# Two transformer blocks on one core: the state space mixer computed transposed, channels on the partitions

## The reference, cut to what matters

```
xbc = silu(conv4(xbc) + conv_b)                  # per channel, along the tokens
xs, bm, cm = split(xbc, [1024, 256])             # 16 heads of 64 channels; 2 groups
dt = softplus(dtb + dt_bias);  a_neg = -exp(a_log)
y = ssd(xs, dt, a_neg, bm, cm)                   # for each head: (C B^T * decay) @ (xs * dt)
y = y + d_skip[:, None] * xs                     # one D for each head
y = y * silu(zb)                                 # the gate z, 1024 channels
y = rmsnorm over each group of 512 channels, eps 1e-5, times norm_g
```

## Time and profile before

| what | us |
|---|---|
| median of three runs | 2783.86 |
| the profiled execution | 2783.81 |
| its span, first to last instruction | 2782.0 |
| PE busy (share of the span) | 2761.5 (99%) |
| DVE busy | 1822.0 (65%) |
| ACT busy | 1464.6 (53%) |
| POOL busy | 239.3 (9%) |

### The profile page before, as it was taken

How to read it: one execution, slowest core, us unless ns; L and a number is a source line. 1 busy time by engine, 2 the same in 40 slices (tenths; PEclk the granted TensorE clock), 3 DMA queues, 4 the chain that set the end, 5 groups by cost and what they waited for, 6 DMA issues and landing times.

```text
span 2782.0 us, 44672 instructions
## 1 busy us (share of the span) xinstructions
PE 2761.5 (99%) x18116; PEld 2471.4 (89%) x18116; DVE 1822.0 (65%) x2860; ACT 1464.6 (53%) x2398; POOL 239.3 (9%) x187
## 2 busy tenths in 40 slices
PE   9999999999999999999999999999999999999998
PEld 8989889989989889989888987899899888878997
DVE  6656676646656666656568777765565687787755
ACT  6445555545455655444456566445454566655452
POOL 0010011010010010010014100110100131001100
PEclk9999999999999999999999999999999999999999
DMA  6544445555544345555555444555555554445653
GB/s 247 197 168 163 149 156 191 190 188 192 202 171 149 139 172 205 202 185 203 195 189 182 139 171 153 212 197 197 191 201 191 182 188 152 160 159 184 217 193 125
DMA packets 75068, 504.09 MB, mean 181 GB/s; under 512 B 8784, under 2 KB 10480, under 8 KB 19184
## 3 DMA queue, kind: packets, MB, share of 16 engines
q1 hardware_dynamic: 74576, 501.07, 50.7%
q10 hardware_dynamic: 288, 0.17, 0.0%
HBM read 500.12 MB, written 1.08 MB: 180 GB/s over the span
## 4 chain that ended last, share of the span: by engine, by line
PE 92%; DVE 5%; POOL 2%; ACT 1%; issue 1%; DMA 0%; SPq 0%; DVEq 0%; ACTq 0%
PE ps L1570 45%; PE ps L1589 39%; PE ps L1610 3%; POOL wlo L2496 2%; DVE wlo L2038 1%; DVE conv L2325 1%; PE ps L1705 1%; PE ps L1703 1%; PE ps L1730 1%; ACT whi L1781 0%; ACT conv L1949 0%; PE ps L1720 0%; PE ps L1721 0%; PE ps L1722 0%; DVE ps L2142 0%
## 5 line engine op out<-in xcount | busy, mean ns | idle before, releaser
L1781 ACT ACTIVATE whi<-raw 128x1024 fp32r<-128x1024 f32 (+3 forms) x938 | 975.9, 1043 | 636.8 <-PE ps L1570 428.8
L2038 DVE TENSOR_TENSOR wlo<-raw,whi 128x1024 fp32r<-128x1024 f32 (+2 forms) x894 | 1083.8, 1219 | 257.5 <-ACT whi L1781 256.5
L1589 PE MATMUL ps<-xT_both,whi 128*128 128x256 f32 x6592 | 824.2, 278 | 1.0 <-DVE v_mla L2252 1.0
L1589 PEld LDWEIGHTS ps<-xT_both,whi 128*128 128x128 f32 x6592 | 783.1, 188 | 8.3 <-issue 6.9
L1570 PE MATMUL ps<-whi,xT_both 128*128 128x512 f32 (+2 forms) x2336 | 628.6, 391 | 2.9 <-DVE xT_both L2061 1.6
L1570 PEld LDWEIGHTS ps<-whi,xT_both 128*128 128x128 f32 x2336 | 425.3, 188 | 84.2 <-issue 9.3
L1589 PE MATMUL ps<-xT_both,wlo 128*128 128x256 f32 x3296 | 442.5, 277 | 0.0
L1589 PEld LDWEIGHTS ps<-xT_both,wlo 128*128 128x128 f32 x3296 | 405.8, 188 | 0.0
L1570 PE MATMUL ps<-wlo,xT_both 128*128 128x512 f32 (+2 forms) x1168 | 354.4, 384 | 0.3 <-DVE wlo L2038 0.3
L1570 PEld LDWEIGHTS ps<-wlo,xT_both 128*128 128x128 f32 x1168 | 218.3, 188 | 43.7 <-DVE wlo L2038 1.4
L1570 PE MATMUL ps<-whi,hT_hi 128*128 128x512 f32 x704 | 221.4, 390 | 0.0
(11 more groups left out here) (310 smaller groups left out, 2210.9 us busy)
## 6 DMA issues: line engine op xcount, KB each, us to landing
raw<-in_w SPq DMA_DIRECT2D x435, 1024.0 KB, 4.8
vr<-in_vrows SPq DMA_DIRECT2D x19, 512.0 KB, 6.1
raw<-in_w SPq DMA_DIRECT2D x12, 768.0 KB, 4.3
raw<-in_w SPq DMA_DIRECT2D x10, 896.0 KB, 4.5
sums<-scratch SPq DMA_DIRECT2D x8, 512.0 KB, 4.5
raw<-in_w SPq DMA_DIRECT2D x4, 832.0 KB, 4.5
raw<-in_w SPq DMA_DIRECT2D x4, 576.0 KB, 3.7
raw<-in_w SPq DMA_DIRECT2D x4, 512.0 KB, 6.9
```

Source lines behind the costliest of these rows:

```text
L1589: made = e.matmul(out, ws[:, o:o + 128], xs[:, kt, :], start=kt == 0 and n == 0 and c % 2 == 0, stop=kt == job.nk - 1 and n == 2, skip_gro ...
L1781: e.activation(out, raw, ACT.Copy).then_inc(*mark("hi", i))
L2038: e.tensor_tensor(out, raw, hi.bitcast(F32), sub).then_inc(*mark("lo", i))
```

## The change

The state space branch stays with channels on the partitions from the convolution to the branch product. The order of the pieces changes: the first chunk of va opens the stage, z follows xbc and is computed in the form `columns`. `ssd` swaps its operands: 64 columns of `xd` are stationary and the decay tiles are streamed, 256 and 128 columns, two heads on the two column halves. D comes in on ACT by channel (`conv_d`), the POOL multiplication by D is gone. The sum of squares over 512 channels now runs over partitions and tiles: ACT squares (`ssd_square`), DVE adds the tiles of a group (`ssd_add`), PE multiplies by a 128x128 tile of 1/512 so that each partition holds the mean of each of 256 tokens (`ssd_mean`), DVE adds eps, POOL takes the power of -0.5 of that 128x256 tile, DVE multiplies the group's 128x1024 of `ob` by it. Group 0 is done at steps s = 12 and 13 of the chain, group 1 in `last_norm` after the last piece of va. `to_T` of `ob` is replaced by `halve_b`, which has no transposes.

```diff
-        for n in (0, 1):
-            gemm(("z", l, n), (l,), 8, [(w, ZB + 512 * n, ZB + 512 * n + 512)])
+        gemm(("va", l, 0), (l,), 8, [(w, VA, VA + 512)])
...
-        for key, at in (("qa", QA), ("ka", KA), ("va", VA), ("qc", QC), ("kc", KC), ("vc", VC)):
-            for n in (0, 1):
+        for key, at in (("z", ZB), ("qa", QA), ("ka", KA), ("va", VA), ("qc", QC), ("kc", KC), ("vc", VC)):
+            for n in (0, 1) if key != "va" else (1,):
...
-            conv.put(acc, ("tr", "conv", l, ct))
+            conv.put(acc, ("act", "conv_d", l, ct))
...
+        for n in (0, 1):
+            banks, free = self.two()
+            outs = [banks[i // 2][:, 256 * (i % 2):256 * (i % 2) + 256] for i in range(4)]
+            tok = self.gemm_w(("z", l, n), xt, 8, outs, free)
+            for j in (0, 1):
+                self.do("z_out", l, n, j, banks[j], tok, self.xn_free)
...
+                    self.do("ssd_square", l, q)
+                if s == 12:
+                    self.do("ssd_add", l, 0)
+                if s == 13:
+                    ssd_mean(0)
...
+        def last_norm():
+            self.do("ssd_add", l, 1)
+            yield
+            ssd_mean(1)
             yield
...
         self.drain()
+        self.spawn(last_norm())
...
-                self.to_T([ob[:, t, :] for t in (0, 1)], fence2[0:2], 8, oT, self.col("ssm_norm_g_2", l, 8))
+                for k in range(0, 8, 2):
+                    key = (oT.name, oT.gen, k)
+                    self.do("halve_b", key, l, k, oT, oT.free, self.col("ssm_norm_g_2", l, 8))
...
# PE
-            e.matmul(ps[:, 64 * j:64 * j + 64], w[:, j, 0:128], xd[:, 0, c], start=True, stop=True)
-            e.matmul(ps[:, 256 + 64 * j:320 + 64 * j], w[:, j, 128:256], xd[:, 0, c], start=True, stop=False)
-            made = e.matmul(ps[:, 256 + 64 * j:320 + 64 * j], w[:, j, 256:384], xd[:, 1, c], start=False, stop=True)
+                e.matmul(ps[64 * i:64 * i + 64, 256 * n:256 * n + 256], xd[:, 0, at_n + 64 * i:at_n + 64 * i + 64],
+                         w[:, 2 * n + i, 0:256], start=True, stop=False)
...
+                made = e.matmul(ps[64 * i:64 * i + 64, 256 * n + 128:256 * n + 256],
+                                xd[:, 1, at_n + 64 * i:at_n + 64 * i + 64], w[:, 2 * n + i, 256:384],
+                                start=False, stop=True)
...
+        pe.wait_ge(*at("vec", "ssd_ss", l, g))
+        e.matmul(ps[:, 0:256], m["part"].broadcast_to([128, 128]), tiles8(m["xn"])[:, 4 * g, :], start=True, stop=True
+                 ).then_inc(*mark("att", "ob", l, g))
...
# DVE
+    def ssd_mean(l, g, ps, free):
+        ve, r = (tiles8(m["xn"])[:, 4 * g + n, :] for n in (1, 2))
+        dve.wait_ge(*at("att", "ob", l, g))
+        e.tensor_scalar(ve, ps[:, 0:256], 1e-5, None, add).then_inc(*mark("msq", "ob", l, g))
+        dve.wait_ge(*at("rstd", "ob", l, g))
+        o = tiles8(m["ob"])[:, 4 * g:4 * g + 4, :]
+        e.tensor_tensor(o, o, bc1(r, 4), mul).then_inc(*mark("vec", "ob", l, g))
...
# POOL
-    def ssd_norm(l, t, ss, ms, r):
-        root(r, ms, "ob", l, t)
+    def ssd_mean(l, g, *_):
+        ve, r = (tiles8(m["xn"])[:, 4 * g + n, :] for n in (1, 2))
+        pool.wait_ge(*at("half"))
+        pool.wait_ge(*at("msq", "ob", l, g))
+        e.tensor_tensor(r, ve, m["phalf"][:, 0:1].broadcast_to([128, 256]), ALU.pow).then_inc(*mark("rstd", "ob", l, g))
```

More of the change, by code:

```diff
@@ L249, in place @@
 def place(key):
-    if key[0] in ("qk1", "xbc", "qc", "kc"):
+    if key[0] in ("qk1", "z", "xbc", "qc", "kc"):
         return COLUMNS_AT
@@ L303, in memory @@
     sbuf("phalf", [128, 2])
+    sbuf("part", [128, 1])
     lined("xT")
@@ L1103, in mixer2, with v_chunk @@
         self.do("rows_in", l, fence)
-        for n in (0, 1):
+        def v_chunk(name, n, dst, mid=None, pre=None):
             banks, free = self.two()
-            toks = self.gemm(("z", l, n), xt, 8, [[(b, 0, 512)] for b in banks], free, None if n else self.between,
-                             pre=self.between_early)
+            toks = self.gemm((name, l, n), xt, 8, [[(b, 0, 512)] for b in banks], free, mid, pre=pre)
             for t in (0, 1):
-                self.do("z_out", l, n, t, banks[t], toks[t], self.xn_free)
-                self.main.put(banks[t], ("gate", "z", l, n, t))
+                there = ("copy_a" if t else "copy_v", name, l, n, t)
+                self.do("bank_out", there, dst[:, t, 512 * n:512 * n + 512], banks[t][:, :], (toks[t],))
+                self.main.put(banks[t], there)
+        v_chunk("va", 0, va, self.between, self.between_early)
         self.run_later()
@@ L1236, in mixer2 @@
             rope_chunk("ka", n, 8)
[L1238 to L1247, removed]
+        v_chunk("va", 1, va)
         self.drain()
+        self.spawn(last_norm())
         fence2 = (("vec", "ob", l, 0), ("vec", "ob", l, 1), ("att", "ssd", l, 3))
@@ L1760, in tensor_program @@
         "scale_row": scale_row, "mla_turn": mla_turn, "rope2_turn": rope2_turn, "conv_out": conv_out, "dt_turn": dt_turn, "qk": qk,
-        "turn_probs": turn_probs, "values": values, "values_T": values_T, "cb": cb, "ssd": ssd})
+        "turn_probs": turn_probs, "values": values, "values_T": values_T, "cb": cb, "ssd": ssd,
+        "ssd_mean": ssd_mean})
 def crow_of(m):
@@ L1968, in decay_exp, with ssd_square, halve_b @@
         e.activation(w, w, ACT.Exp).then_inc(*mark("act", "decay_exp", l, q))
-    def ssd_norm(l, t, ss, ms, r):
[L1971 to L1976, removed]
+    def ssd_square(l, q):
+        for n in (0, 1):
+            act.wait_ge(*at("vec", "ssd_y", l, q, n))
+        e.activation(pair8(m["xn"], q), pair8(m["ob"], q), ACT.Square).then_inc(*mark("sumsq", "ob", l, q))
+    def halve_b(key, l, k, oT, free, gain):
+        act.wait_ge(*at("vec", "ob", l, k // 4))
+        for f in free:
+            act.wait_ge(*at(*f))
+        for j in (k, k + 1):
+            made = e.activation(oT.H[:, j, :], tiles8(m["ob"])[:, j, :], ACT.Copy, scale=gain[:, j:j + 1])
+        made.then_inc(*mark("xhi", *key))
     def rope2(name, l, n, t, bank, tok, buf, free):
@@ L2359, in ssd_out @@
         dve.wait_ge(*at("att", "ssd", l, q))
[L2360 to L2375, removed]
+        for n in (0, 1):
+            k = 2 * q + n
+            o = tiles8(m["ob"])[:, k, :]
+            dve.wait_ge(*at("act", "conv_d", l, k))
+            e.tensor_tensor(o, o, ps[:, 256 * n:256 * n + 256], add).then_inc(*mark("vec", "ssd_sum", l, q, n))
+            dve.wait_ge(*at("vec", "ssd_sum", l, q, n))
+            dve.wait_ge(*at("gate", "z", l, k // 4, k % 4 // 2))
+            e.tensor_tensor(o, o, tiles8(m["xn"])[:, k, :], mul).then_inc(*mark("vec", "ssd_y", l, q, n))
@@ new lines, in ssd_add, with ssd_mean @@
+    def ssd_add(l, g):
+        z = tiles8(m["xn"])
+        for q in (2 * g, 2 * g + 1):
+            dve.wait_ge(*at("sumsq", "ob", l, q))
+        step(e.tensor_tensor(pair8(m["xn"], 2 * g), pair8(m["xn"], 2 * g), pair8(m["xn"], 2 * g + 1), add))
+        e.tensor_tensor(z[:, 4 * g, :], z[:, 4 * g, :], z[:, 4 * g + 1, :], add).then_inc(*mark("vec", "ssd_ss", l, g))
+    def ssd_mean(l, g, ps, free):
+        ve, r = (tiles8(m["xn"])[:, 4 * g + n, :] for n in (1, 2))
[4 more added lines that the diff above has]
+        e.tensor_tensor(o, o, bc1(r, 4), mul).then_inc(*mark("vec", "ob", l, g))
@@ L2377, in vector_program, with halve_b @@
+    def halve_b(key, l, k, oT, free, gain):
+        dve.wait_ge(*at("xhi", *key))
+        for j in (k, k + 1):
+            made = e.scalar_tensor_tensor(out=oT.L[:, j, :], in0=tiles8(m["ob"])[:, j, :], scalar=gain[:, j:j + 1],
+                                          in1=oT.H[:, j, :].bitcast(F32), op0=mul, op1=sub)
+        made.then_inc(*mark("xlo", *key))
     rotated = []
```

61 lines of the change are left out of this document (39 added, 22 removed).

## The result

The changed kernel takes 2940.07 us (median of 4, 2938.43 to 2940.61) against 2783.88: a ratio of 1.0561, 95% interval 1.0548 to 1.0573. The profiled execution took 2939.65 us, its span is 2937.5.

A forecast was written before the change was run, and what follows sets the result against it. PE, busy 99% of the span, was taken to bound the kernel: 2783.8 - 8.6 of PE work + 135.6 of waits for POOL's power = 2910.8, so 2911 us; the 8-in-10 range was 2800 to 2955.

The forecast's parts named there:

- rival A: The forecast: POOL's wide power grows 0.14 to 0.19 us a column, 37 to 48 us, time 2911 to 2954; chance 0.58.
- the power's duration: POOL's power on 128x256: 0.554 us plus 255 columns at 0.144, so 37.3 us each.
- the count of the waits: PE idle behind the power: 34.9 us at group 0, 32.9 at group 1, 135.6 over both layers.
- the edits at nothing: Opening va chunk, conv_d on ACT, DVE additions, z's place: priced at nothing, a wait at the convolution bounded at 1 us.
- the PE work: Matmul work on PE: ssd -8.7, ob transposes -3.5, ssd_mean +2.0, z as columns +1.6; sum -8.6 us.
- B: Rival: POOL's power is pipelined in a long tile, 6 to 30 us; with 17 us, time 2830; chance 0.20.
- C: Rival: POOL's long power is cheap, under 5.6 us; PE's lead covers most, 2775 us, 0.3% faster; chance 0.17.
- 4P - 13.6: PE idle at the four powers over both layers, P being one power's duration: 135.6 us.
- The lead: PE work in hand after the mean's matmul, before it stands: 11.6 us at group 0, 12.1 at group 1.

The follow-up runs named there:

- e9: Changed kernel plus unread matmuls (292, 44 and 294) in a free bank at three places where PE idles, output unchanged: 2933.53 us.
- e1: Changed kernel with POOL's power taken of one column only, repeated for all tokens (the other tokens' norm left out): 2778.31 us.
- e2: Changed kernel with the power on 64 columns, the norm of the other tokens left out: 2817.6 us.
- e10: Changed kernel with the power on 128 columns, half of the norm left out: 2857.8 us.
- e11: Transposed form with the root on 128x2 and later group 0 mean, both matmuls of one head written before the other's: 2777.89 us.

## Why the prediction was right, point by point, and where its sizes were off

It said 2911 us, by rival A, and measured were 2940. The mechanism and the order of the waits are as forecast, and the time lies in the range that A gave, 2885 to 2955. The difference of 29 us comes out of these terms, 15.3 for the power's duration, 11.2 for what the count of the waits misses, 3.5 for the edits at nothing, less 1.5 for the PE work:

- **The power's duration.** 37.3 us by 0.144 a column from one and two columns; it is 41.13, by 0.159. That is 4 x 3.8 = 15.3 us, the largest error. The step from the first to the second column was a tenth too low for a long tile; B (pipelined) and C (the multiply's pace) are wrong altogether, and the line has no bend from 64 to 256 columns. That the step between one and two columns would hold for 255 was a guess, with 0.58 on it, and no row ahead of the result could have shown it; the two steps read there, 0.144 and 0.186, lie on either side of what was measured. The floor that the Trainium skill gives for two inputs (GPSIMD Engine Reference, 3.1, Elementwise) agrees with the multiply of this kernel and says nothing of the power, which costs some seventy times the multiply: 0.159 us a column against 2.3 ns.
- **The lead, and DVE's queue.** 4P - 13.6 gives 150.9 with the real P, and the powers cost 162.1. PE's lead is as counted (11.7 and 12.2 us). What the count has wrong is that DVE adds eps as soon as the mean's matmul ends: at group 0 it does so 2 us later. With the full clock (e9) this is most of the 4.6 us that the clock leaves of the surplus. PE's idle time grew by 150.8 over that of the kernel before; that this is so near 150.9 is chance, since 3.5 of it belong to other edits and part of PE's slow work stands where waits were counted. I had put group 0 at the second piece of ka 0; it is at that of ka 1, since `ssd()` is now appended to the chain behind z. The pieces behind it are of the same kind in both places, so this changed no term, which was luck and not insight.
- **The clock.** It was no term of the sum. TensorE's clock falls to half in these waits and stays there for some matmuls after them: 6.6 us on the path, by e9. I looked for what is late next on the engines and not for what the clock of a waiting PE does.
- **PE work.** Forecast -8.6, measured -10.1 us busy (e1). The products took 1.45 us a q in place of 1.60, since the bubble comes once, which saves 8 x (2.69 - 1.45) = 9.9 in place of 8.7; the mean's matmul 0.45 in place of 0.5; 24 matmuls of z's form 2.83, as forecast.
- **Edits at nothing.** New idle time of 3.5 us in e1 is what they cost: 2.0 for the mean, which asks for DVE's sum too early, 1.4 for a transpose behind a rotation's copy. I had bounded a wait at the convolution by 1 us; PE's wait there is 0.5 us over both layers in the kernel before, 0.4 in e1 and 0.9 in the changed kernel.

Together: 2783.8 - 10.1 + 3.5 = 2777.2, which is e1's profiled execution at 2777.5; plus the 162.1 of the powers 2939.3, against 2939.65.

## What to carry to other kernels

Before an operation is moved to a wider tile, take its price per column from two widths of that very operation: one instruction of 0.7 us became one of 41. A wait in order costs what stands behind it on the engine; here some 12 us of matmuls were all that PE had in hand. Count the queue of the waiting engine from what already stands in it. When a norm's statistic lies along the free axis on all partitions, take the root while it is small and spread it afterwards; two short matmuls did that at under half a microsecond a group.

## What the runs showed of the hardware that I had not expected

- POOL's power of fp32 costs 0.159 us for each column of 128 partitions from 64 columns to 256, with 0.55 for the first (e1, e2, e10 and the changed kernel).
- PE's clock was at half after waits of 2.5 to 4.5 us as after those of 33 to 35 us, and PE's work was stretched by about the same: 14.5 us in e2 and 14.8 in the changed kernel, for the waits at the four powers. At full width 6.6 us of it were on the path (e9).
- Two column halves of the array take their matmuls from one instruction stream independently: in e11 the second head's first pass ran together with the first head's, though two matmuls of the first head stand before it in the program.
